# Reordering the 64 experts of a routed feed-forward layer: the 128-slot experts spread among the larger ones

## The reference, cut to what matters

```
def swiglu(x, wg, wu, wd):
    return (jax.nn.silu(x @ wg) * (x @ wu)) @ wd
...
    def run_block(args):
        tok, wt, e = args
        xb = xs_pad[tok]
        return swiglu(xb, w_e_gate[e], w_e_up[e], w_e_down[e]) * wt[:, None].astype(xb.dtype)
...
    return routed + swiglu(xs, w_s_gate, w_s_up, w_s_down)
```

## Time and profile before

| | us |
|---|---|
| median of 3 runs | 2686.42 (2684.85 to 2686.94) |
| the profiled execution | 2686.19 |
| its span, first to last instruction | 2684.4 |
| start of the experts' stage on TensorE (first half tile of L2598) | 1784.2 |
| first gate_up of an expert | 1825.1 |
| end of the last down projection | 2656.2 |

### The profile page before, as it was taken

How to read it: one execution, slowest core, us unless ns; L and a number is a source line. 1 busy time by engine, 2 the same in 40 slices (tenths; PEclk the granted TensorE clock), 3 DMA queues, 4 the chain that set the end, 5 groups by cost and what they waited for, 6 DMA issues and landing times. The chain is left out here.

```text
span 2684.4 us, 35226 instructions
## 1 busy us (share of the span) xinstructions
PE 2526.3 (94%) x12288; PEld 1688.3 (63%) x12288; DVE 1040.9 (39%) x2279; ACT 599.5 (22%) x1175; POOL 778.8 (29%) x582
## 2 busy tenths in 40 slices
PE   6999999999799999989979989889999999999995
PEld 3566666665555555556645645447777777777774
DVE  3233334545243333229964226534233333332221
ACT  2223333333143333210013101100112222211111
POOL 1000000000044344300000005434555666555452
PEclk9999999999899999989989999999999999999998
DMA  8111111010342221062112161038989999999996
GB/s 262 45 42 51 39 35 40 29 37 22 86 118 61 77 76 52 22 191 60 36 48 64 36 211 56 17 123 288 296 279 330 329 325 329 323 337 365 366 364 198
DMA packets 213118, 406.88 MB, mean 152 GB/s; under 512 B 57464, under 2 KB 140718, under 8 KB 196471
## 3 DMA queue, kind: packets, MB, share of 16 engines
q1 hardware_dynamic: 168382, 314.39, 34.1%
q0 software_dynamic: 28704, 74.32, 11.1%
q10 hardware_dynamic: 15856, 15.92, 1.8%
HBM read 343.53 MB, written 72.83 MB: 155 GB/s over the span
## 5 line engine op out<-in xcount | busy, mean ns | idle before, releaser
L2371 POOL DMA_INDIRECT mergedT<-tokens_normed,gather_rows x308 | 312.6, 1015 | 122.0 <-issue 95.2
L2561 PEld LDWEIGHTS pGe<-xT,we_g 128*128 128x128 f32 x2048 | 272.6, 191 | 47.0 <-issue 23.6
L2561 PE MATMUL pGe<-xT,we_g 128*128 128x160 f32 (+2 forms) x2048 | 285.8, 298 | 10.0 <-DVE xT L2472 9.9
L2561 PE MATMUL pUe<-xT,we_u 128*128 128x160 f32 (+2 forms) x2048 | 280.3, 295 | 0.0
L2561 PEld LDWEIGHTS pUe<-xT,we_u 128*128 128x128 f32 x2048 | 273.6, 191 | 0.0
L2472 DVE STREAM_TRANSPOSE xT<-mergedT 128x1280 f32<-128x1280 f32 (+2 forms) x64 | 154.4, 2412 | 264.6 <-DMA mergedT<-tokens_normed,gather_rows 264.5
L1374 PE MATMUL pKs<-ws_uk,cTs 128*128 128x512 f32 x512 | 251.7, 636 | 1.2 <-issue 1.2
L805 PE MATMUL pFill<-hT,fill_w 128*128 128x344 f32 x768 | 239.5, 456 | 7.1 <-ACT fill_out L514 7.0
L1109 POOL TENSOR_TENSOR rk<-ssk,half 128x32 f32<-128x32 f32 x32 | 173.3, 5427 | 233.0 <-DVE ssk L1229 233.0
L2571 PE MATMUL pYe<-we_d,h_e 128*128 128x512 f32 x512 | 230.1, 592 | 0.0
L805 PEld LDWEIGHTS pFill<-hT,fill_w 128*128 128x128 f32 x768 | 141.7, 190 | 83.7 <-issue 21.8
(11 more groups left out here) (415 smaller groups left out, 3078.0 us busy)
## 6 DMA issues: line engine op xcount, KB each, us to landing
we_g<-in_w_e_gate SPq DMA_DIRECT2D x64, 1024.0 KB
we_u<-in_w_e_up SPq DMA_DIRECT2D x64, 1024.0 KB
we_d<-in_w_e_down SPq DMA_DIRECT2D x64, 1024.0 KB
mergedT<-in_cache_latent SPq DMA_DIRECT2D x96, 128.0 KB, 2.1
raw_columns<-fill_out SPq DMA_DIRECT2D x48, 172.0 KB
fill_w<-in_w_in SPq DMA_DIRECT2D x16, 512.0 KB
branch_w<-in_w_in SPq DMA_DIRECT2D x11, 512.0 KB
mergedT<-tokens_normed,gather_rows POOLq DMA_INDIRECT x308
```

Source lines behind the costliest of these rows:

```text
L2371: pool.indirect_dma_start(out=xg[v % 2][:, g, :], out_offset=None, in_=quarter, in_offset=bass.IndirectOffsetOnAxis(ap=gi[v % W][:, g:g + ...
L2561: mm = pe.matmul(dst[p][:, f * CAP:f * CAP + n], w[r][:, k, f * P:(f + 1) * P], xT[p][:, k, 0:n], start=k == 0, stop=k == KD - 1)
```

## The change

The 24 light ranks are spread evenly over the 64 positions. `RANK_AT[u]` is the rank that position `u` processes; each class keeps its own order. In groups of eight positions the pattern is H H L H H L H L. The heavy ones at positions 0 to 17 have 192 slots, those from position 19 on have 160. Positions 2, 5, 7, 10 and so on to 63 are light. Because a light expert now comes at position 2, SyncE reads all three tables before any weights, and VectorE calls `other_rows` in `start`, between add_ring(0) and gather_ring(2). The counts of tails that the waits use are computed from `CAPS`.

```
-    CAPS = [c for c, n in RANK_CAPS for _ in range(n)]
+    LIGHT = RANK_CAPS[-1][1]
+    ranks = {False: iter(range(NE - LIGHT)), True: iter(range(NE - LIGHT, NE))}
+    RANK_AT = [next(ranks[(u + 1) * LIGHT // NE > u * LIGHT // NE]) for u in range(NE)]
+    CAPS = [[c for c, n in RANK_CAPS for _ in range(n)][rank] for rank in RANK_AT]
...
-            return bass.ds(eng.value_load(keep.order[0:1, u:u + 1], min_val=0, max_val=NE - 1), 1)
+            return bass.ds(eng.value_load(keep.order[0:1, RANK_AT[u]:RANK_AT[u] + 1], min_val=0, max_val=NE - 1), 1)
...
         def tails(u):
-            return min(u, TAILS)
+            return sum(c > P for c in CAPS[:u])
...
                     tables(q, NGS[:1], "table_in")
+                    tables(q, NGS[1:], "tables_in")
 
                 def load(q, u):
                     r = u % W
-                    if u == 1:
-                        tables(q, NGS[1:], "tables_in")
...
-                        pool.wait_ge(S["y_vec"], 1 + TAILS * q + u + 1)
+                        pool.wait_ge(S["y_vec"], 1 + TAILS * q + tails(u) + 1)
...
-                    for u in range(3):
+                    for u in range(2):
                         gather_ring(u)
                     add_ring(0)
+                    other_rows(q)
+                    gather_ring(2)
...
-                    if u == 2:
-                        other_rows(q)
...
-                        pe.wait_ge(S["y_vec"], TAILS * q + u + 1)
+                        pe.wait_ge(S["y_vec"], TAILS * q + tails(u) + 1)
```

More of the change, by code:

```diff
@@ L2478, in gate, with other_rows @@
                     v.tensor_tensor(h[p][:, :, 0:n], sg[p][:, :, 0:n], pU[p][:, 0:2 * CAP].rearrange("p (f n) -> p f n", f=2)[:, :, 0:n], ALU.mult).then_inc(S["h_ready"], 1)
+                def other_rows(q):
+                    v.wait_ge(S["tables_in"], 16 * (len(NGS) - 1) * (q + 1))
+                    for n in NGS[1:]:
+                        rows(q, n)
+                    v.wait_ge(S["rows_ready"], len(NGS) * (q + 1))
+                    v.sem_inc(S["passed"], 1)
                 def start(q):
@@ L2515, in start @@
                         v.sem_inc(S["passed"], 1)
[L2517 to L2522, removed]
                 def body(q, u):
```

## The result

The kernel with the change takes **2671.34 us** (median of 5 runs, 2669.37 to 2675.3), against 2686.42 before (5 runs beside them, 2684.85 to 2689.94). The ratio is 0.9944, with a 95% interval of 0.9929 to 0.9958: 11 to 19 us faster. The forecast was 2679.3 us, the range 2673.5 to 2690.5. The profiled execution took 2670.31 us, its span 2668.5.

What follows compares the result with a forecast made beforehand. TensorE, busy 94% of the span, was taken as the bound, losing 13.1 us to late gathers among light experts. Terms -12.7 + 4.1 + 1.2 + 0.5 = -6.9 us on 2686.19 gave 2679.3 us, range 2673.5 to 2690.5.

Steps and rivals of the forecast that it cites:

- Part 1: Light experts: levelling traffic removes TensorE's waits for late gathers, -12.7 us, with 0.4 us of stalls left where gathers bunch.
- Part 2: Table work on VectorE in `start` delays half tile 8 by 7.0 us; a later 2.9 us gap absorbs part: +4.1 us.
- Part 4: SyncE in `start`: two table transfers ahead of position 0's weights cost nothing; a small transfer could move a fraction of a microsecond.
- Part 3: TensorE's clock in `start`: a longer stand before half tile 8 costs more time at the lower clock, +1.2 us.
- Part 5: End of the stage: with a heavy second last expert, the last tail lands later, +0.5 us, between -0.5 and +2.
- The chain of landings: Rival, chance 0.19: GpSimd's loop of accumulating transfers, not traffic, is the bound; 11.5 us of stalls stay, 2690.4 us.
- the longer heavy loops: Rival, chance 0.10: heavy experts' GpSimd loops stretch to 14.1 us beside more traffic, adding 34 us of stalls, 2712.9 us.
- The table work is hidden: Rival, chance 0.12: something else holds TensorE's start in `start`, so table work and clock terms vanish, 2674.0 us.

Runs made afterwards that it cites:

- e6: Kernel before, but light experts load no down matrix and reuse the one left in the buffer; 2674.64 us, one execution.
- e10: The change plus a further 0.39 MB transfer per expert from position 4 on; 2689.34 us, one execution.
- e9: The change with the two other tables issued again behind the first weights, table work still in `start`; 2674.34 us, one execution.
- e5: Kernel before, with SyncE waiting for the primer to land before issuing position 0's weights; 2682.3 us, one execution.
- e11: e4 with position 0's weights held until the primer lands, those from position 2 on until gather 0 lands; 2672.77 us, ratio 0.9946.
- e2: Kernel before with only a new order: first eight positions heavy, lights spread over the other 56, old `start`; 2669.96 us, ratio 0.9932.
- e1: The change's `start` (tables first, table work on VectorE there) with the old order of experts; 2684.47 us, ratio 0.9993.
- e7: The change with light experts in six runs of four instead of an even spread; 2680.74 us, one execution.
- e12: The change itself run again, unaltered; 2670.82 us, ratio 0.994 to the kernel before.
- e13: e11 with the weights from position 1 on, not 2, held until gather 0 lands; 2669.9 us, ratio 0.9939.
- e14: e11 with all weights held until gather 0 lands, without the wait for the primer; 2668.7 us, ratio 0.9928.
- e3: Kernel before with only the two other tables read ahead of the first weights, table work left at position 2; 2684.47 us, ratio 0.9991.
- e4: e2's order with all tables read ahead of the weights, table work left at position 2; 2672.47 us, ratio 0.9943.

## Why the prediction was wrong in size and right in kind

**Part 1, the light stalls, right.** Forecast -12.7, bounds 0 and -13.1; measured -13.07. No bunching remained, so the 0.4 us kept for it was not needed. The budget (pace times rate, group by group) was borne out at 347 GB/s, e6 shows traffic as the cause by taking some away, and e10, as far as it goes, agrees from the other side.

**Part 2, table work in `start`, wrong: +4.1 forecast.** The size of the table work was right, 7.06 us. But "so that start moves to 1809.7" took the beginning of VectorE's work as fixed. It began 3.53 us sooner against S, so half tile 8 moved not by 7.0 but by 3.40 (S+18.54 to S+21.94). "The gathers of positions 0 and 1 are issued as before" fell with it: the first was issued at S+13.22 in place of S+16.46, and turn(0) came at S+27.97 in place of S+30.18, with its gather already there. The gap of 2.94 us before half tile 14 was gone, as forecast. The part's own rule, 7.0 - 2.9, holds once the 3.5 us are put in, and e9, without them, shows +3.45 against the same execution of before.

**Part 4, SyncE, is the step that failed.** It put the early tables at "nothing", and said that the small transfer "could move by a fraction of a microsecond". That transfer moved by the 3.5 us: with 0.14 MB of tables ahead of them, the weights come too late to stand in the primer's way, which e5 shows from the other side. I had the row's releaser (the primer) and did not ask what the primer itself waited behind.

**Part 3, the clock, wrong: +1.2 forecast, 0 measured.** The stand became four times as long, 7.94 us in place of 2.04, and the eight matmuls behind it took 5.39 us, as before 5.40. Windows of `start`, after:
```profile
1798.00:1803.00 5.00, 0.00 (x0) 0.00 (x0) 4.05 (x21) 0.00 (x0) 3.78 (x5) 0.71 1.04 426
1803.00:1808.00 5.00, 4.52 (x7) 2.04 (x8) 2.91 (x5) 0.00 (x0) 3.80 (x4) 0.61 1.01 389
```
The granted clock was at its lower level already before the work came (0.50 from 1801 to 1803, when TensorE stood), and that cost no more than before, where it was 0.94 from 1802 to 1803 and 0.50 from 1803 to 1806. The rule that I cited from the Trainium skill ("TensorE: Matmul & The Clock Gate", section "What's actually happening") would have made it dearer, as I read it; this trace does not.

Parts 2 to 4 together: forecast +5.3, measured +0.18, and -2.3 to -2.5 against the two other executions of the old `start`. These 5.1 us or more are the largest part of the miss.

**Part 5, the end.** Forecast +0.5 within -0.5 to +2; measured -0.36, within the range and within the scatter of this stretch. The last accumulate starts 8.13 us after that of the expert before, as against 7.25, but 5.0 us after TensorE's end (2640.69), as against 5.4 before:
```profile
2637.59 1.57 POOL L2393 DMA_INDIRECT sums<-mergedT,add_rows  x1 [8.95 <-ACT mergedT L2428]
...
2645.72 1.57 POOL L2393 DMA_INDIRECT sums<-mergedT,add_rows  x1 [4.91 <-DMA sums<-mergedT,add_rows]
```

**The rivals.** The chain of landings, my 0.19, and the longer heavy loops are refuted: in e6 the loop follows TensorE down to 10.58 us, and in the change no gate_up waits. The figure of about 425 GB/s (the Trainium skill, "HBM Reference", section "Specifications (TRN2)"), which spoke for the chain, is not reached where gathers and accumulates run beside the weights: 362 to 366 GB/s at share 1.03 was all. In `start`, without accumulates, the windows above show 426 and 389. What lowers the rate was not varied by itself. "The table work is hidden", my 0.12 at 2674.0, is what happened in effect, though TensorE was not held by something else: half tile 8 did wait for the addition. With its -12.7 and +0.5 at their measured -13.07 and -0.36 it gives 2672.8.

**The range.** Its lower end, 2673.5, was the rival's value with nothing around it. The profiled execution also had 2.65 us of scatter ahead of the stage in its favour; without them it would be at 2672.96, still below the range. The three runs shown (2.1 us apart) hid that executions of one kernel spread over 10 us.

## What to carry to other kernels

Make a budget of traffic per item, pace times rate, from a stretch that stalls and one that doesn't; if the stalls' side is at the ceiling and the mean is 5% below it, alternating the items can remove the stalls, as it did here. With the light items in runs of four, stalls were left; runs of two and three were not tried. Before you cost work added to a waiting engine, follow the releaser back once more: what do the small transfers it waits for queue behind, and which later wait would have taken the same time? And when an experiment against your theory fails, look in the queues whether the suspect was really gone.

## What the runs showed of the hardware

- **The traffic ceiling.** With 1 MB matrices, gathers of 128 quarter rows and accumulating transfers together, 362 to 366 GB/s at DMA share 1.03 (before, e10). In `start`, without accumulates, windows at share 1.00 to 1.04 show 361 (before) to 428 GB/s (e11, 1798 to 1803). That the accumulates make the difference is not shown.
- **Small transfers beside weights.** The addition that waits for the primer (2 x 4 KB) started 6.6 to 7.1 us after the primer's issue with weights behind one table (before, e2, e6, e9), 3.6 to 4.2 with three tables ahead of the weights (after, e1, e7, e12), 2.6 with one table and the weights held back (e5), and 3.9 to 4.4 with three tables and the weights held back (e11, e13, e14). The first gather took 8.97, 5.82 and 4.64 us from its last issue with 6, 3 and 0 MB of weights let through before it, and 7.7 us with nothing held back (e3, e4).
- **The clock after a stand.** Stands of 2.04, 7.94 and 9.02 us before half tile 8 cost 1.8 to 2.05 us alike (eight matmuls in 5.40, 5.39 and 5.65 against 3.60). Stands of 1.42 to 1.92 us there cost 0.1 (3.70, in e3, e4, e5, e11, e13, e14), but so did one of 2.25 us before half tile 4 of before (3.70). Before half tile 14, 2.94 us cost 0.1 (before), 4.36 us cost 1.84 (e2: 2.85 and 2.75 for two groups that take 1.88), and 3.77 and 6.45 us cost 3.1 and 3.2 (e5, e11). So the length of a stand alone doesn't give its cost. Timeline of PE, e2:
```profile
1816.80 2.85 PE L2602 MATMUL pZe<-w_sd,shared_hT 128*128 128x512 f32 x4 [4.36 <-DVE mergedT L2501]
1819.44 2.75 PE L2602 MATMUL pUe<-w_sd,shared_hT 128*128 128x512 f32 x4
```
- **Scatter of one `start`.** Between before and e2, which have the same `start`, S to G differs by 2.6 us (40.91 and 43.55): e2 stands 1.4 us longer before half tile 14 and then loses 1.7 us more to the clock, and was 0.5 us ahead until there.
